# Two transformer blocks on one core: the value product of attention is put off by one more item

## What is computed

```python
# layers 0 and 1: 8 heads of 64, worked on in 4 pairs
s = einsum('bqgrd,bkgd->bgrqk', qg, k) * HEAD_DIM ** -0.5
p = softmax(s);  out = einsum('bgrqk,bkgd->bqgrd', p, v)
# layers 2 and 3: 8 heads, two softmax maps each, values 128 wide
p = softmax(einsum('bqhcd,bkhcd->bhcqk', qi, keys) * scale)
w = p[:, :, 0] - lam * p[:, :, 1]
out = einsum('bhqk,bkhv->bqhv', w, vals);  out = rmsnorm(out, sub_g) * (1 - lam_init)
```

## Time and profile before

| | |
|---|---|
| median of 3 runs | 2439.39 us (2436.88 to 2440.82) |
| the profiled execution, its own time | 2440.44 us |
| span of that execution | 2438.6 us |
| TensorE busy | 2330.7 us, 96% of the span |
| VectorE, ScalarE busy | 1312.5 us (54%), 1074.6 us (44%) |
| granted TensorE clock, mean of the span | 0.984 |
| first and last scores of layer 0, 1, 2, 3 (us) | 85 to 193, 668 to 731, 1036 to 1366, 1949 to 2135 |

### The profile page before, as it was taken

The page is one execution under the profiler, slowest core; times in us unless marked ns, Lnnn a source line. Parts: engine busy times, 40 slices in busy tenths (PEclk is TensorE's granted clock), DMA queues, the critical chain, the costliest instruction groups (busy, mean ns, idle before and its releaser), DMA issues.

```text
span 2438.6 us, 37310 instructions
## 1 busy us (share of the span) xinstructions
PE 2330.7 (96%) x14812; PEld 1924.5 (79%) x14812; DVE 1312.5 (54%) x2326; ACT 1074.6 (44%) x2076; POOL 33.8 (1%) x40
## 2 busy tenths in 40 slices
PE   6999999999888999999999999999999999999999
PEld 3657877777857899867666788888888887799999
DVE  4544533333655456577776434534335678756665
ACT  3443522222545345544445523522323755655543
POOL 0300000000100000000000000000000000000000
PEclk8999999999999999999999999999999999999999
DMA  7564333333344765344554322233333221154554
GB/s 279 173 227 145 101 115 116 118 121 111 105 156 131 254 211 165 104 147 156 199 175 163 106 97 91 70 112 104 112 112 112 88 87 61 61 165 147 182 182 147
DMA packets 94892, 336.05 MB, mean 138 GB/s; under 512 B 10624, under 2 KB 12672, under 8 KB 94464
## 3 DMA queue, kind: packets, MB, share of 16 engines
q1 hardware_dynamic: 94720, 333.67, 40.6%
HBM read 332.58 MB, written 1.05 MB: 137 GB/s over the span
## 4 chain that ended last, share of the span: by engine, by line
PE 84%; DVE 6%; ACT 5%; DMA 3%; issue 2%; SPq 0%; ACTq 0%; DVEq 0%
PE out L1352 23%; PE out L1353 22%; PE out L1354 22%; DMA raw<-stream 3%; PE sc L1417 2%; DVE w_lo L1742 2%; PE pt L1427 1%; PE pt L1306 1%; PE pv L1443 1%; ACT w_hi L1482 1%; PE sc L1306 1%; PE aux L1286 1%; ACT e_t L1639 1%; PE out L1306 1%; PE pv L1441 1%
## 5 line engine op out<-in xcount | busy, mean ns | idle before, releaser
L1352 PE MATMUL out<-act_hi,w_lo 128*128 128x512 f32 (+1 forms) x2144 | 747.1, 348 | 19.9 <-DVE act_lo L1921 5.0
L1353 PE MATMUL out<-act_lo,w_hi 128*128 128x512 f32 (+1 forms) x2144 | 732.8, 342 | 0.0
L1354 PE MATMUL out<-act_hi,w_hi 128*128 128x512 f32 (+1 forms) x2144 | 732.0, 341 | 0.0
L1482 ACT CAST w_hi<-raw 128x1024 fp32r<-128x1024 f32 (+2 forms) x444 | 452.2, 1022 | 452.1 <-PE out L1354 415.2
L1742 DVE TENSOR_TENSOR w_lo<-raw,w_hi 128x1024 fp32r<-128x1024 f32 (+2 forms) x444 | 528.8, 1194 | 114.9 <-ACT w_hi L1482 114.8
L1352 PEld LDWEIGHTS out<-act_hi,w_lo 128*128 128x128 f32 x2144 | 410.9, 192 | 82.8 <-issue 27.6
L1354 PEld LDWEIGHTS out<-act_hi,w_hi 128*128 128x128 f32 x2144 | 410.5, 191 | 46.0
L1353 PEld LDWEIGHTS out<-act_lo,w_hi 128*128 128x128 f32 x2144 | 410.9, 192 | 43.1
L1352 PE MATMUL out<-mix_hi,w_lo 128*128 128x256 f32 (+1 forms) x1186 | 391.0, 330 | 3.8 <-DVE mix_lo L1764 2.2
L1353 PE MATMUL out<-mix_lo,w_hi 128*128 128x256 f32 (+1 forms) x1186 | 388.1, 327 | 0.0
L1354 PE MATMUL out<-mix_hi,w_hi 128*128 128x256 f32 (+1 forms) x1186 | 387.9, 327 | 0.0
(11 more groups left out here) (245 smaller groups left out, 2332.9 us busy)
## 6 DMA issues: line engine op xcount, KB each, us to landing
raw<-stream SPq DMA_DIRECT2D x604, 512.0 KB, 3.5
raw<-stream SPq DMA_DIRECT2D x16, 384.0 KB, 3.2
raw<-stream SPq DMA_DIRECT2D x16, 256.0 KB, 2.6
x<-xin SPq DMA_DIRECT2D x1, 2048.0 KB, 11.8
consts<-const SPq DMA_DIRECT2D x1, 1344.0 KB, 7.1
x<-ctx SPq DMA_DIRECT2D x1, 1024.0 KB, 5.7
out<-x SPq DMA_DIRECT2D x8, 128.0 KB, 1.7
consts<-const SPq DMA_DIRECT2D x1, 320.0 KB, 11.6
```

Of the source, the lines that this page charges most:

```text
L1352: nc.tensor.matmul(ps, wl, xh, start=(k == 0), stop=False)
L1353: nc.tensor.matmul(ps, wh, xl, start=False, stop=False)
L1354: ins = nc.tensor.matmul(ps, wh, xh, start=False, stop=(k == s.nk - 1))
L1482: nc.scalar.copy(w_hi[:, number % HL, 0:n], raw[:, place[number] % RAW, 0:n]).then_inc(S["hi_ready"], 1)
```

## The change

A second item is kept back: besides `before` (the item one back) there is `older` (the item two back). Right behind the scores of an item come the value product and the outputs of the item two back; then `E` of this item, and then the transposes of the item before. Nothing stands between the two parts of fills but `N`. At the end of a layer's attention the rest of the last two items is done in order.

```diff
             scores(item)
+            if older:
+                values(older)
+                outputs(older)
+            step("E", item=item)
             if before:
                 turn_probs(before)
-            step("E", item=item)
             part(2 * j)
             pump(units - units // 2)
             normalize(item)
-            if before:
-                values(before)
             part(2 * j + 1)
             pump(units // 2)
-            if before:
-                outputs(before)
-            before = item
+            older, before = before, item
...
     def attend_last():
-        nonlocal before
+        nonlocal before, older
+        values(older)
+        outputs(older)
         turn_probs(before)
         values(before)
         outputs(before)
...
-            last["v", h % 2] = ("pv_done", c.get("pv_done", 0) + 1)
+            last["v", h % 2] = ("pv_done", c.get("pv_done", 0) + 2)
```

More of the change, by code:

```diff
@@ L318, in attend @@
             normalize(item)
-            if before:
-                values(before)
             part(2 * j + 1)
             pump(units // 2)
-            if before:
-                outputs(before)
-            before = item
-    before = None
+            older, before = before, item
+    before, older = None, None
     def attend_last():
-        nonlocal before
+        nonlocal before, older
+        values(older)
+        outputs(older)
         turn_probs(before)
```

## The result

The change made the kernel slower by a little more than a quarter of a per cent. In the first comparison its median was 2446.13 us (2438.34 to 2454.19, 20 runs) against 2440.89 us before (2435.66 to 2443.39, 20 runs): ratio 1.0027, 95% interval 1.0019 to 1.0035. In microseconds that is 5 to 7, where +1.8 was forecast. The time lies within the range of 2432 to 2449; the effect, 0.27%, is just above the 0.2% (4.9 us) that the prediction called no change.

The account below looks back on a forecast made before the run. TensorE, busy 96% of the span, was taken as the bound, with 39.1 us of attention gaps reachable. Terms -2.3, -0.2, +2.6, +2.4, +0.3, -1.6, +0.6 summed to +1.8 us: 2442.2 profiled, median 2441, range 2432 to 2449.

Parts of the forecast that it names:

- T behind a PV, layers 0 and 1: -2.3: Last items of layers 0 and 1: an older value product covers the probability transposes' wait for normalizing, -2.3 of 2.5 us.
- Layer 3: +2.6: Layer 3: probability transposes' waits go, -2.8 us, but back transposes in six heads wait 0.9 each, +5.4; net +2.6.
- Layer 1: +2.4: Layer 1: ScalarE's copies, now behind the exponentials, delay sums, Fourier products and scores in several items, +2.4 us.
- -1.1 for its last item: Layer 1's last item: a value product covers the probability transposes' wait for normalizing, about 1.1 us.
- Layer 2, T: -0.2: Layer 2: the probability transposes' 3.4 us wait stays; two waits of 1.4 shrink slightly, -0.2 us in all.
- The ends of layers 2 and 3: +0.6: Last value product of layers 2 and 3 waits longer for a copy queued behind another ScalarE read, +0.3 us each.
- DMA: -1.6: Layer 2, ahead of new heads: a longer value product shortens waits for modulation weights at four places, 0.4 us each.
- The clock rival: Layer 1's longer gaps at the fourth and fifth items each bring a clock fall, 6.8 us together, 2448; chance 0.20.
- That the fills absorb it (0.17): VectorE's hidden slack removes layer 3's +5.4 and layer 1's +2.4 us, giving -6.0, 2433; chance 0.17.
- The weight load rival (0.03): Gaps at the probability transposes, counted on the weight load, are lost time: up to 30 us goes, 2411; chance 0.03.

Follow-up runs that it names:

- the repeat: The change itself, unaltered, measured and profiled once more against the kernel before: 2444.94 us against 2439.32, ratio 1.0027.
- back transposes behind T: The change, with layer 3's back transposes (second to seventh head) moved behind the next head's first transposes of the probabilities: 2442.71 us, ratio 1.0016 to before.
- a kernel at 0.9987: Kernel before, with new order in layer 0, layer 1's last item, and last-but-one value product behind the last transposes in layers 2 and 3: 2434.69 us.
- the one at 1.0035: The change, with layer 2's modulation products spread otherwise over a head's eight places: 2447.56 us, ratio 1.0035 to the kernel before.

## Why the prediction was right, and where it failed

T's waits in all, forecast to fall from 11.5 to about 5 us, fell to 6.2, and to 5.8 in the repeat, all of them in layer 2. Term by term:

**T behind a PV, layers 0 and 1: -2.3.** Right. The wait for the normalizing (2.5 us) does not appear after the change. Layer 0's gaps fell from 6.2 to between 2.9 and 5.5, by how long the landings in it took; two waits of the scores for the exponentials there (0.6 us) and part of the last product's wait (1.3, then 0.7) went too.

**Layer 3: +2.6.** Right, wait by wait. T's waits went from 2.8 to nothing, and these rows came (timeline of layer 3 after the change, the place of the earlier trace rows):

```profile
2034.91 1.09 PE L1287 MATMUL aux<-consts,n_r 128*64 128x128 f32 x16
2035.93 0.66 PE L1381 MATMUL pt<-consts,vf 128*128 128x128 f32 x4
2036.05 0.69 DVE L1963 TENSOR_TENSOR k_t<-qg,aux 128x512 f32<-128x512 f32 x1 [0.69 <-PE aux L1287]
...
2037.04 0.42 DVE L2032 TENSOR_TENSOR o_t<-o_t,o_r 128x256 f32<-128x256 f32 x1
2037.52 0.44 PE L1450 MATMUL aux<-consts,o_t 128*128 128x128 f32 x2 [0.93 <-DVE o_t L2032]
2037.88 1.13 PE L1418 MATMUL sc<-k_t,q_t 64*128 64x512 f32 x4
2038.94 1.16 PE L1444 MATMUL pv<-v_t,p_t 128*128 128x128 f32 x8
```

From the rows at 2034.91 the scaled output is ready 2.55 us later, as before (2.6), and TensorE is there 0.93 too early. Five waits of 0.93 and one of 0.87 make 5.5, forecast 5.4; the layer's gaps rose by 2.8. What the forecast did not have is the layer's end, where L1273 and L1287 wait 2.24 and 1.97 us instead of 2.61 and 0.96 together, +0.6, and what followed on it. Granted clock there, after the change and then before it (us, PE, PEld, DVE, ACT, POOL busy, PEclk, DMA share, GB/s):

```profile
2123.20:2130.10 6.90, 6.15 (x29) 6.15 (x30) 4.60 (x14) 5.86 (x12) 0.00 (x0) 0.51 0.24 78
```

```profile
2127.20:2130.60 3.40, 3.04 (x14) 3.04 (x15) 2.33 (x8) 2.51 (x4) 0.00 (x0) 0.50 0.39 143
2130.60:2134.10 3.50, 3.50 (x31) 3.50 (x31) 2.62 (x7) 3.40 (x7) 0.00 (x0) 1.00 0.00 0
```

The low level (0.5, 1.2 GHz) lasts 6.9 us where it lasted 3.4: at half the full level (2.4 GHz) that is some 1.7 us more. Ahead of both falls TensorE was busy but for the waits at L1273 and L1287 (L1272 and L1286 before), and each fall began within the second of them. In the stretch from 1940 to 2175 us the low level takes 10.2 us in all six traces with the new order in layer 3, the repeat among them, and 6.8 in all seven others. That it is so regular speaks for a cost of the order and against chance. How it comes about is not shown. The sum is regular and the place is not: of the seven with the old order, three have one fall of 6.8 us in place of two of 3.4, and one of them (layer 0 and the last item of layer 1) has it at the same waits, 2.61 and 0.96 us, as the kernel before. And of the six with the new order one has three falls of 3.4 (back transposes behind T). No run changed these waits alone. The Trainium skill (TensorE: Matmul & The Clock Gate, "A second HAM failure mode: psum-queue depth-cycling") tells of a kernel whose short idle times between groups of matmuls come often enough that the clock goes up and down. The rows here agree only in kind: one pair of waits, of some 2 us each, stands at the fall.

**Layer 1: +2.4 against -1.1 for its last item, so +1.3.** The mechanism was right, the size a little high. The fifth item's sums wait 1.47 us (0.62 in the earlier trace rows), forecast 1.8; the fourth's Fourier transposes wait 1.43 for the copies, and 0.46 and 0.33 behind them, 2.2 for 1.78 before, as forecast; the third's sums wait 0.4. The layer's gaps rose by 0.4 in all. With the old order in its other items they are 9.2 to 9.3, so these cost up to 0.9; but the term of -1.1 for the last item did not show there by itself (9.8 before, 9.3 in the kernel with layer 0 alone, 9.3 with the last items alone).

**Layer 2, T: -0.2.** It came out at 0, and at -0.4 in the repeat: 6.2 us in five waits, or 5.8 in four, instead of 6.2 in three.

**The ends of layers 2 and 3: +0.6.** Wrong sign, small: 2.0 us instead of 2.9 in both executions of the change.

**DMA: -1.6. This is the step that failed**, and it made a forecast of "no change" out of a loss. The prediction said: "The landing doesn't depend on PE at that point, and the item before now holds a four-tile PV instead of a two-tile one". The first half holds nearly; the second counted the wrong interval. At the first of the four places, 1167 us, the forecast came true: the wait is 1.88 us after the change and was 2.38. At the other three it grew. The second place, ahead of a head of layer 2, before the change (the view of the first row ends within its group, so it counts ten of sixteen products):

```profile
1197.48 0.77 PE L1286 MATMUL aux<-consts,n_r 128*64 128x128 f32 x10
...
1199.05 1.16 PE L1443 MATMUL pv<-v_t,p_t 128*128 128x128 f32 x8
...
1202.98 1.04 PE L1306 MATMUL pt<-raw,cv 128*2 128x256 f32 x16
1203.96 0.71 PE L1443 MATMUL pv<-v_t,p_t 128*128 128x128 f32 x4
1204.94 0.61 PE L1306 MATMUL pt<-raw,cv 128*2 128x256 f32 x8 [0.27 <-DMA raw<-stream]
```

and after it:

```profile
1190.08 1.09 PE L1287 MATMUL aux<-consts,n_r 128*64 128x128 f32 x16
...
1193.84 1.16 PE L1444 MATMUL pv<-v_t,p_t 128*128 128x128 f32 x8
...
1195.58 1.05 PE L1307 MATMUL pt<-raw,cv 128*2 128x256 f32 x16
1197.84 0.61 PE L1307 MATMUL pt<-raw,cv 128*2 128x256 f32 x8 [1.21 <-DMA raw<-stream]
```

From the spread rows to the product that waits there were two value products, of four and of two tiles. Now there is one, of four: the two-tile one of this stretch is put off to the next head. TensorE arrives 1204.94 - 0.27 - 1197.48 = 7.19 us behind the rows before, and 1197.84 - 1.21 - 1190.08 = 6.55 after, 0.64 earlier; the landing came 7.46 and 7.76 us behind them, 0.3 later, though its request had gone out 2.82 us behind the rows instead of 3.77. Together that is the 0.94 by which the wait grew.

The prediction also had nothing at all for the bank, since it took the one such wait of before (2.6 us) for fixed. Before the change a value product stood exactly between the last product of a bank and the first of the next:

```profile
1186.85 0.61 PE L1306 MATMUL pt<-raw,cv 128*2 128x256 f32 x8
1187.39 1.16 PE L1443 MATMUL pv<-v_t,p_t 128*128 128x128 f32 x8
1188.48 0.61 PE L1306 MATMUL pt<-raw,cv 128*2 128x256 f32 x8
```

and the same place after it, with VectorE:

```profile
1179.12 0.61 PE L1307 MATMUL pt<-raw,cv 128*2 128x256 f32 x8
...
1179.80 0.72 DVE L1790 STREAM_TRANSPOSE stage<-pt 128x512 f32<-128x512 f32 x1 [0.26 <-PE pt L1307]
...
1180.58 0.61 PE L1307 MATMUL pt<-raw,cv 128*2 128x256 f32 x8 [0.84 <-DVE stage L1790]
```

The product had covered VectorE's 0.72 us of transposing. Without it 0.84 us are new here, the next border's wait grew from 2.63 to 3.54, and a third one has 0.29. So a term of -1.6 was +1.8 for the landings and +2.1 for the bank: +3.9, 5.5 us off. The bank's part is the firm one: 2.6 us in all seven traces with the old order of layer 2, and 4.4 to 4.7 in all five with the new one and the same places of the modulation products. The landings took 4.6 to 7.3 us in the seven and 7.5 to 8.9 in the five, so their part can be anything from nothing to 4 us between two single traces, 2.4 by the means. With +3.9 in its place the forecast's sum is 1.8 + 5.5 = +7.3, beside the 5 to 7 measured; the ends and layer 1, both dearer in the forecast than in the trace, can be the rest. The kernel with layer 2 as before shows that these waits come from the order of layer 2. That the lost cover makes them is read from the traces, since no run put a product back between two users of the bank and changed nothing else. The place could be read in the trace of before: a value product between two equal rows of L1306.

**The rivals.** The clock rival had 0.20, for layer 1's two gaps. Of the eight traces with the value product put off in all of layer 1 three have a low level there, of 3.4 us each, for instance in the kernel with layer 2 as before, after a 1.47 us gap:

```profile
717.50:720.90 3.40, 3.40 (x17) 1.90 (x16) 1.39 (x2) 0.00 (x0) 0.00 (x0) 0.50 0.59 211
```

That is half of the length of the fall that the rival was priced by the earlier trace rows, in three of eight executions: well under 1 us on average. The five traces with the old order in layer 1, or with it but for the last item, have none there. The mean granted clock was 0.9833 over the runs of the change in the second comparison, and 0.9839 over the runs of before beside them (0.9826 for the change in the first, where the clock of only one run of before is on record). By an estimate from these means, a difference of 0.0006 of 2440 us, the clock has some 1.5 us of the 5 to 7, about what layer 3's end costs. The loss is mostly waits, with a share of clock. That the fills absorb it (0.17) fell with the six waits of L1450. The weight load rival (0.03) fell as well: its busy time hardly moved (1924.5 to 1926.1), and the time followed the gaps of the matmuls. The Trainium skill (Perfetto Trace Analysis, opening note) calls matmul busy time a bad measure and points to the weight load. For how full the engine is nothing here tests that. For the differences between the kernels of these thirteen traces the gaps between matmuls were the better guide: the weight load was busy 1929.5 us in a kernel at 0.9987 and 1925.4 in the one at 1.0035.

**The profiled execution.** What the forecast could not show is how far one execution may lie from its kernel's median. Of the change two were profiled, 4.8 us apart in span, with nearly the same gaps in layers 2 and 3. Their gaps over the whole span are 107.9 and 108.2 us, and the low clock takes 76 and 83 us, so most of the difference is clock. Against the execution of before that does not work: its gaps are 105.1 and its low clock 76 us, as in the first of the change, and still its span is 0.9 us longer, as TensorE is busy 3.6 us more there. Why is open.

## What to carry to other kernels

Before an instruction is moved, look not only at what waits in its new place, but at every pair of neighbours that it stands between today: a product between two users of one bank, or between two users of landed buffers, is cover even where the trace shows no wait, and its loss appears as a new one. Count the cover between two fixed points (the release and the user), not for an item as a whole. Where the other engine's chain sets the time between two points, as VectorE's from the spread rows to T here, the order of the first engine only chooses where it waits. A change that goes through all layers is best tried layer by layer: here the halves were worth about -4 us (some of it perhaps clock) and +10 us.

## What had not been expected of the hardware

At the end of layer 3 the low clock lasted 3.4 us longer in every trace with the new order than in every trace without it (10.2 against 6.8 us, six traces and seven), although in the change the waits ahead of it differed by only 0.6 us in sum (2.24 and 1.97 against 2.61 and 0.96). At half the clock these 3.4 us cost some 1.7, about three times the difference of the waits. That the waits are the cause is not shown.

A request that goes out sooner need not land sooner. The block of 512 KB that TensorE waited for at 1204.94 us before the change was asked for 2.07 us after the one ahead of it and landed 3.65 us later; the same block after the change was asked for 1.13 us after the one ahead and took 4.89 us (requests at 1199.18 and 1201.25, then at 1191.77 and 1192.90). This is one pair, and no rule of the distance: the blocks around these took 3.2 to 5.8 us, and one that was asked for 1.52 us after the one ahead took 5.21.
